# Reordering query preparation and moving three weight splits from VectorE to GpSimd in a fused four-layer fp32 kernel

## What is computed

```
proj = u @ w_in                       # many 128-column tiles
qa = rope(qa); ka = rope(ka); qi = rope(qi); ki = rope(ki)      # sparse branch (8 heads)
score = sum_h w_idx[h] * relu(qi_h @ ki)                        # index score, causal
idx   = top_k(score, 128)                                       # keys each query may see
o_a   = softmax(qa @ ka[idx]) @ va
qb = rope(qb)                                                   # block branch (8 heads, 2 groups)
kc, vc = gelu(blocks(k_c) @ w1) @ w2, gelu(blocks(v_c) @ w1) @ w2
o_b = g0 * softmax(qb @ kc) @ vc + g1 * selected(qb, k_s, v_s) + g2 * window(qb, k_w, v_w)
h   = h + concat(o_a, o_b) @ w_out
```

## Time and profile before

| | |
|---|---|
| median of 3 runs | 1956.84 us |
| lowest to highest | 1955.66 to 1967.98 us |
| the profiled execution | 1955.66 us |
| its span, first to last instruction | 1953.9 us |
| mean granted TensorE clock over the span | 0.979 of full |
| PE busy | 95% of the span |
| DVE, ACT, POOL busy | 50%, 41%, 24% |

### The profile page before, as it was taken

How to read it: one execution, slowest core, us unless ns; L and a number is a source line. 1 busy time by engine, 2 the same in 40 slices (tenths; PEclk the granted TensorE clock), 3 DMA queues, 4 the chain that set the end, 5 groups by cost and what they waited for, 6 DMA issues and landing times.

```text
span 1953.9 us, 24545 instructions
## 1 busy us (share of the span) xinstructions
PE 1850.2 (95%) x9658; PEld 1466.3 (75%) x9662; DVE 979.8 (50%) x1598; ACT 799.8 (41%) x1407; POOL 467.7 (24%) x471
## 2 busy tenths in 40 slices
PE   6999998997999989999999999999999899999997
PEld 5987777773677746667888888877877788888885
DVE  5345554586446587843533334354565354333334
ACT  4235663346435445554442323233444434232322
POOL 0035551100312225442120102004556302110200
PEclk9999999998999989999999999999999799999999
DMA  4221111221012410001232222221111023322222
GB/s 153 97 76 54 44 44 56 85 87 44 1 38 89 135 55 23 23 23 34 91 103 98 97 97 97 97 91 61 55 65 54 12 87 107 98 96 98 97 97 75
DMA packets 40289, 143.32 MB, mean 73 GB/s; under 512 B 4592, under 2 KB 4976, under 8 KB 40176
## 3 DMA queue, kind: packets, MB, share of 16 engines
q1 hardware_dynamic: 40176, 141.76, 21.8%
HBM read 139.64 MB, written 2.10 MB: 73 GB/s over the span
## 4 chain that ended last, share of the span: by engine, by line
PE 83%; DVE 7%; ACT 5%; POOL 2%; issue 2%; DMA 1%; DVEq 0%; SPq 0%; ACTq 0%; POOLq 0%
PE BANK L268 21%; PE BANK L270 21%; PE BANK L269 21%; PE BANK L844 2%; PE BANK L617 2%; PE BANK L1470 2%; PE BANK L1427 1%; PE BANK L1451 1%; ACT WH L245 1%; DVE LH L707 1%; PE BANK L898 1%; PE BANK L602 1%; DVE WL L254 1%; PE BANK L2209 1%; PE BANK L2156 1%
## 5 line engine op out<-in xcount | busy, mean ns | idle before, releaser
L245 ACT ACTIVATE WH<-WRAW 128x1024 fp32r<-128x1024 f32 x262 | 273.4, 1045 | 465.4 <-PE BANK L270 423.2
L254 DVE TENSOR_TENSOR WL<-WRAW,WH 128x1024 fp32r<-128x1024 f32 (+1 forms) x249 | 323.1, 1298 | 266.6 <-ACT WH L245 265.0
L268 PE MATMUL BANK<-HH,WH 128*128 128x512 f32 x1048 | 426.3, 407 | 20.0 <-DVE WL L254 17.7
L270 PE MATMUL BANK<-HL,WH 128*128 128x512 f32 x1048 | 410.4, 392 | 0.0
L269 PE MATMUL BANK<-HH,WL 128*128 128x512 f32 x1048 | 410.0, 391 | 0.0
L268 PEld LDWEIGHTS BANK<-HH,WH 128*128 128x128 f32 x1048 | 198.0, 189 | 69.8 <-ACT WH L245 18.4
L269 PEld LDWEIGHTS BANK<-HH,WL 128*128 128x128 f32 x1048 | 198.2, 189 | 43.1 <-issue 5.3
L270 PEld LDWEIGHTS BANK<-HL,WH 128*128 128x128 f32 x1048 | 197.7, 189 | 42.4
L2097 POOL TENSOR_TENSOR HID<-TMP,HID 128x512 fp32r<-128x512 f32 x64 | 82.9, 1296 | 525.8 <-ACT HID L2078 525.8
L268 PE MATMUL BANK<-HID,WH 128*128 128x512 f32 x512 | 199.2, 389 | 0.0
L269 PE MATMUL BANK<-HID,WL 128*128 128x512 f32 x512 | 199.2, 389 | 0.0
(11 more groups left out here) (373 smaller groups left out, 3167.8 us busy)
## 6 DMA issues: line engine op xcount, KB each, us to landing
WRAW<-in_w SPq DMA_DIRECT2D x77, 512.0 KB, 3.4
WRAW<-in_wu SPq DMA_DIRECT2D x64, 512.0 KB, 3.3
WRAW<-in_wd SPq DMA_DIRECT2D x64, 512.0 KB, 3.2
WRAW<-in_w0o SPq DMA_DIRECT2D x8, 512.0 KB, 3.5
WRAW<-in_w1o SPq DMA_DIRECT2D x8, 512.0 KB, 3.5
WRAW<-in_wc SPq DMA_DIRECT2D x8, 512.0 KB, 3.3
WRAW<-in_w2o SPq DMA_DIRECT2D x8, 512.0 KB, 3.3
WRAW<-in_w3o SPq DMA_DIRECT2D x8, 512.0 KB, 3.4
```

What stands on the lines that cost most here:

```text
L245: e.activation(WH[b % NS][:, 0:n], WRAW[b % NR][:, 0:n], ACT.Copy).then_inc(*inc("s_high", ("high", b)))
L254: e.tensor_tensor(WL[b % NS][:, 0:n], WRAW[b % NR][:, 0:n], WH[b % NS][:, 0:n].bitcast(F32), ALU.subtract).then_inc(*inc("s_low_pool" if p ...
L268: e.matmul(dst, ah, bh, start=first and i == 0, stop=False)
L270: made = e.matmul(dst, ah, bl, start=False, stop=last and i == len(sets) - 1)
```

## The change

Five edits, all in layer 2 ("e"):

1. POOL instead of DVE makes the low parts of the weight blocks e9, e10 and e11.
2. DVE: `index_sum(3)` moves from step 1 of the loop to just before the loop.
3. ACT: `high(E_Q)` moves from before `gelu(1)` to behind the sigmoid and the table load.
4. POOL: `gelu_low(1)` moves ahead of `cos(E_Q)`.
5. POOL, in each step of the loop: `cos` of the turning tile moves ahead of `scale` and `low`.

```diff
-                   if block["e", 12] <= b <= block["e", 14] + NS and name not in ("wc1", "wc2")
+                   if block["e", 9] <= b <= block["e", 14] + NS and name not in ("wc1", "wc2")
                    or b == block["e", 3]}
@@ l2_vector
             c_keys(1)
             split("wc2", 1)
+            index_sum(3)
             for step in range(E_STEPS):
...
-                if step == 1:
-                    index_sum(3)
                 if step == 2:
                     c_values()
@@ l2_scalar
             keys(1)
-            high(E_Q)
             gelu(1)
             e.activation(gates, gates, ACT.Sigmoid).then_inc(*inc("s_gates", ("gates",)))
             e.preload_act_table_set("natural_log_exp_and_others")
+            high(E_Q)
             split("e", E_Q + 1)
             split("wc2", 1)
@@ l2_gpsimd
             cos(E_KW)
+            gelu_low(1)
             cos(E_Q)
-            gelu_low(1)
             low(E_Q)
             split("e", E_Q)
             split("e", E_Q + 1)
             split("wc2", 1)
             w.wait_ge(*at("gates"))
             for step in range(E_STEPS):
+                if e_turning(step) is not None:
+                    cos(e_turning(step))
                 if 0 <= step - 3 < E_N:
                     scale(step - 3)
                 if e_turning(step - 1) is not None:
                     low(e_turning(step - 1))
-                if e_turning(step) is not None:
-                    cos(e_turning(step))
                 if e_ended(step) is not None:
                     split("e", e_ended(step))
```

## The result

| | before | after |
|---|---|---|
| median of 9 runs, same chip | 1965.58 us | 1981.71 us |
| lowest to highest | 1955.66 to 1968.40 us | 1971.79 to 1984.64 us |
| the profiled execution | 1955.66 us | 1976.83 us |
| its span | 1953.9 us | 1975.0 us |
| mean granted clock | 0.979 | 0.970 |

The ratio is 1.0088, with a 95% interval of 1.0065 to 1.0110: slower by 0.9%, within 1% as forecast, but 17 us above the predicted 1964.7 and outside the range (1957 to 1971).

What follows compares the result with a forecast made beforehand. PE, busy 95% of the span, was taken as the bound: only its waits or clock count. Entry -0.7, turnings +6.7 and clock +3.0 gave +9.0 on 1955.66, or 1964.7 us; range 1957 to 1971.

Steps and rivals of the forecast that it cites:

- The turnings' term: Loop steps 8, 15, 22, 36, 43: the earlier cosine product goes straight into PE's wait for POOL's scaling, 6.7 us lost.
- Step 29: The turning in the loop where DVE scales the unit to transpose and POOL has only the cosine product: 0 us lost.
- ACT's split of e11: Loop's entry: stands ahead of the first exponential, waits for its block's load until 718.5, then takes 1.05 us.
- The entry, "-0.7": Loop's entry, edits 1 to 4: first transposes at 728.65 instead of 729.36, 0.7 us gained; bounds 4.5 gain, 1.3 loss.
- The first exponential "at 719.6": Loop's entry: starts behind a late load and ACT's split at 719.6, against 719.45 before; DVE's maximum ready about 718.
- "This costs nothing by itself": Loop's entry: first scores slip from 711.77 to about 712.8 at no cost, as PE then waits for the first exponential anyway.
- The clock, "3.0": Behind the turnings: longer PE waits bring two of four possible new half-clock stretches, 3.0 us lost; bounds 0 to 6.0.
- My price of 1.5 us for one stretch: Behind a turning: one half-clock stretch, 3.6 us long in the old trace, was counted as 1.5 us lost.
- The rule on oscillation: Turnings: gaps between matmul bursts bring back half clock each time, so all four new falls would come, 1967.7 us.
- The base, 1955.66: Whole kernel: profiled execution's time, to which the +9.0 us was added; fastest of three runs, 1.2 us below their median.
- The late reload: Rival, loop's entry: the weight block's load or the query's high part comes later; entry +1.3 to +3, about 1967.5 us; chance 0.12.
- The rival with long half-clock stretches: Turnings: each of five longer waits leads to some 3.5 us lost at half clock, 1979.2 us; chance 0.03.

Runs made afterwards that it cites:

- cos_only: Kernel before with only POOL's cosine product moved ahead of the scaling in turning steps: loop 185.5 us against 173.8, ratio 1.0038.
- no_cos: Changed kernel with POOL's cosine product put back behind the scaling: entry 46.0 us, loop 173.8 us, ratio 0.9986.
- splits_high: Kernel before with the three low parts on POOL and the query's high part behind the table load: entry 45.1 us, ratio 0.9992.
- splits_only: Kernel before with only the low parts of three weight blocks moved from DVE to POOL: entry 41.2 us against 44.7, ratio 0.9986.
- index_only: Kernel before with only index_sum(3) moved ahead of the loop: entry 46.8 us, loop 172.3 us, ratio 1.0000.
- after_fill: Changed kernel plus unread matmuls on PE in the five turnings' waits: loop 178.8 us against 186.7; ratio 1.0027 against the kernel before.
- loop_new: Kernel before with the loop's low parts made by DVE behind the turning step's reciprocals, not by POOL: loop 176.7 us, ratio 1.0013.
- candidate: Kernel before with three low parts on POOL, index_sum(3) in step 2, tile 8's cosine product ahead of the last low part: entry 44.3 us, ratio 0.9972.
- splits_index: Kernel before with the three low parts on POOL and index_sum(3) ahead of the loop: entry 43.4 us, ratio 0.9994.

## Why the prediction was wrong, point by point

**What was right.** The direction, and that it stays within 1%; that POOL's scaling ends PE's wait at the turnings, so `cos` goes straight into it (cos_only against no_cos). The five waits were forecast at 2.2, 3.0, 2.1, 2.0 and 2.8 us and measured at 2.14, 3.44, 2.06, 1.93 and 2.70. The turnings' term: predicted 6.7 us, measured 14.3 - 6.7 = 7.6. Step 29 itself added nothing, as forecast; the 1.0 us behind it at 844.62 was not foreseen. In the entry, the first scores: predicted 712.8, measured 720.39 - 8.0 = 712.4. ACT's split of e11: predicted 718.5, waiting for the transfer, measured 718.6.

**The entry, "-0.7", was +1.5.** The step that failed is DVE's time ahead of the first exponential.
- *The first exponential "at 719.6".* It came at 721.7 (729.69 - 8.0), and these 2.1 us are nearly the whole miss of 2.2: the transfer's chain before it and PE's 7.45 us behind it (731.28 to 738.60, 7.3) were as forecast. I had let DVE gain its lead and finish `index_sum(3)` in 3.4 us; it took 8.1, as its additions met POOL's two low parts. I had weighed a collision for the last addition only, at 0.7 us. The page "SBUF — State Buffer" of the Trainium skill, section "Who interferes with whom", says that a DVE instruction with two SBUF inputs and a GpSimd instruction that reads SBUF contend for a port pair that one of them locks; the trace agrees, and for the three-operand additions too: 0.75 us and 0.80 us each became 1.66 and 2.70. The rule should have been applied to every DVE row beside the new POOL work.
- *"This costs nothing by itself", of the stall moved behind `high(E_Q)`.* This did not make the miss, because with edit 2 the first exponential's wait hides the stall. But it was not true of edit 3 by itself: splits_high against splits_only lost 3.9 us, by the late reload, and by PE's stall and half clock, for which DVE waits. I had not asked what edit 1 would give without edit 3: 3.5 us, which was thrown away.

The sizes interact: edit 2's 2.1 us are there alone and vanish behind edit 3. Summing edits one by one would not have given +1.5 either.

**The clock, "3.0", was about 5.4.** The loop lost 13.0 us, of which 7.6 are the waits; the rest goes with 17.1 us more at half clock (23.9 against 6.8). The step that failed was the count. I took two new falls of 3.6 us, 7.2 us in all. There were four new ones, at steps 8, 22, 36 and 43, the one at step 8 of double length, and the one at step 15 doubled; the one at step 29, which I had not seen in before, went. I had written that PE's timeline has no gap of note between the places that I listed, but at step 29 it has one of 2.42 us with half clock behind it. Six score matmuls of 512 columns took 1.65 us behind step 8 and behind step 43 (897.35 in the timeline). I said I'd be wrong if more than one stretch lasted beyond 4 us; two did. My price of 1.5 us for one stretch held: it is what index_only's loop has less than before's for one stretch fewer. Times five it is 7.5 us, of which about 2 didn't reach the end of the loop; where they went stays open. The rule on oscillation in "TensorE: Matmul & The Clock Gate" of the Trainium skill, section "HAM oscillation — how this bites in real kernels", by which I had all four falls, 1967.7 us, and which I had set at half weight, fits the count: all five turnings had a fall, and after_fill, which fills the gaps, leaves 3.4 us at half in the loop. It is no law here: the waits of 2.4 us at step 29 are alike in both kernels, and only before's was followed by a fall.

**The base, 1955.66, was not the kernel's usual time.** This is the largest part. Against its own base the sum missed the layer by 5.5 us: 2.2 in the entry, 0.9 at the turnings, 2.4 in the clock. The other 9.9 us are the distance from the profiled execution to before's median over nine runs, 1965.58, and 1.6 is left, within what the ratio is uncertain (0.22%, 4.4 us, to either side). With that median as base the same forecast of +9.0 would have read 1974.6. Two of three runs had stood near 1956 and the third at 1967.98, and I built on the first; over nine runs two are below 1957. The spread of 12 us in three runs was the sign: it is wider than the whole term that I forecast, and the range should have held it.

**The rivals.** None came in whole. The late reload's size for the entry was met (+1.3 to +3, measured +1.5), but its cause was not the transfer: DVE's maximum ended last. The rival with long half-clock stretches was right that all five waits would lead to one, and wrong in their length: two of 6.8 and three of 3.4 us, where it had five of 8.3.

## What to carry to other kernels

When work is put ahead of the instruction that another engine already waits for, all of it goes into that wait, and where the waiting engine is TensorE count the clock's fall behind it as well, here 5 us on top of 8. When low parts or other elementwise work move to GpSimd, go through every DVE row in SBUF that will stand beside it, not only the last; here that turned 3.4 us into 8.1. And a base needs its spread: if three runs lie 12 us apart, a sum that is exact to 1 us on one of them says little about the median.

## What the hardware showed

**Half clock that outlasts its wait.** The 8 us before the layer, and most of the spread of the profiled executions, come from layers that no edit touches. At 480 us PE has a wait of about 3 us for DVE in both kernels, before first, then after:

```profile
480.63 1.08 PE L970 MATMUL BANK<-mqr,CF 128*128 128x512 f32 x1 [3.04 <-DVE mkr L1058]
...
480.65 2.04 PE L970 MATMUL BANK<-mqr,CF 128*128 128x512 f32 x2 [3.27 <-DVE mkr L1058]
```

Behind it the clock was at half for 3.4 us in before and for 23.9 us in after. The window 480 to 530 us, in before:

```profile
480.00:530.00 50.00, 49.37 (x239) 28.79 (x239) 23.25 (x81) 24.33 (x66) 15.97 (x25) 0.97 0.00 1
```

and in after:

```profile
480.00:530.00 50.00, 49.35 (x189) 26.47 (x189) 18.98 (x66) 20.44 (x55) 12.59 (x20) 0.76 0.00 1
```

PE was busy 99% in both, but in after 24 us of the 50 were at half clock (50 x 0.24 x 2), and 50 fewer matmuls were done. Over the stretch up to the last key tile the profiled executions had 17.1 us at half clock (before, splits_high, loop_new) or 20.5 (candidate, splits_index), and reached the tile at 699.1 to 701.5 us, or 41 to 58 us at half clock (all others), and reached it at 707.2 to 716.7. The code up to there is the same in all. Which group an execution lands in is not set by the kernel: before's 31 runs on one chip went from 1956.25 to 1969.28. What decides it stays open: no run varied those layers. The share of runs in the faster group, four of ten against three of 31, makes about half of candidate's 0.9972; with before's share its mean would be some 0.9988 of before's. Within each group its runs are also 1.7 to 2.5 us faster on the mean, for which the stretches show only 0.5.

**DVE beside GpSimd.** Single instructions on data in SBUF took up to eight times as long beside a GpSimd low part (0.29 to 2.33 us), and the GpSimd side lost as well (two low parts 5.55 us instead of 4.7), while in after a search step of 0.41 us (MATCH_REPLACE8, 728.12, one input) and the maximum of 1.22 us (728.44, from a bank) beside the low part at 727.78 (2.34 us) took no longer than elsewhere.
